# Expert weights loaded as one 16 KB run per partition in a two-layer mixture-of-experts kernel

## The reference

```
g = sel.reshape(sel.shape[:-1] + (N_GROUPS, EXPERTS_PER_GROUP))      # 16 experts in 4 groups
...
_, idx = lax.top_k(masked, TOP_K)                                    # 2 experts for each token
...
for e in range(N_EXPERTS):
    hid = jax.nn.silu(h @ w_gate[e]) * (h @ w_up[e])                 # (256,1024) @ (1024,512), twice
    out = out + gate[..., e:e + 1] * (hid @ w_down[e])               # (256,512) @ (512,1024)
```

## Time and profile before

| what | value |
|---|---|
| median of three runs | 2164.47 us |
| the profiled execution's own time | 2157.56 us |
| its span, first to last instruction | 2155.8 us |
| mean granted TensorE clock | 0.888 of full speed |
| TensorE matmuls busy | 1800.6 us |
| VectorE busy | 833.1 us |
| ScalarE busy | 460.8 us |
| DMA packets | 153206, 348.00 MB |
| DMA rate over the span | 161 GB/s |

### The profile page before, as it was taken

One profiled execution on the slowest core, in us unless ns is written; L12 is line 12 of the kernel. 1 busy time (PEld: TensorE's weight loads), 2 busy tenths in 40 slices (PEclk: granted clock), 3 DMA queues, 4 the chain that ended last, 5 costly groups with the idle time before them and its releaser, 6 DMA issues.

```text
span 2155.8 us, 23213 instructions
## 1 busy us (share of the span) xinstructions
PE 1800.6 (84%) x9255; PEld 1241.6 (58%) x9259; DVE 833.1 (39%) x1792; ACT 460.8 (21%) x812; POOL 0.4 (0%) x6
## 2 busy tenths in 40 slices
PE   6868899999695799999679876776789988687998
PEld 5545444434564454344265555775389984447998
DVE  7943211101404311001263465555255553505665
ACT  1031111111113111111011421110134430313443
POOL 0000000000000000000000000000000000000000
PEclk9858899999895889999879768887989998888999
DMA  8051379999304238999920000001525434101551
GB/s 278 0 215 52 107 269 393 396 395 356 128 30 185 90 131 311 396 392 395 342 101 27 1 1 0 1 1 37 198 73 196 160 120 153 40 0 40 182 208 59
DMA packets 153206, 348.00 MB, mean 161 GB/s; under 512 B 8096, under 2 KB 15136, under 8 KB 153136
## 3 DMA queue, kind: packets, MB, share of 16 engines
q1 hardware_dynamic: 145616, 338.28, 42.6%
q10 hardware_dynamic: 7520, 8.75, 1.3%
HBM read 345.97 MB, written 1.05 MB: 161 GB/s over the span
## 4 chain that ended last, share of the span: by engine, by line
PE 66%; DVE 13%; DMA 10%; issue 4%; ACT 4%; SPq 2%; another core or an unknown queue 1%; DVEq 1%; ACTq 0%
PE ps L690 62%; DMA ring<-in_w_up 9%; DVE ring L1634 2%; SPq L601 2%; DVE arena L1634 2%; DVE bias L1640 1%; DVE h L1640 1%; PE ps L964 1%; PE ps L697 1%; ACT arena L1444 1%; PE ps L1007 1%; DVE small L1640 1%; DMA arena<-in_rel_bias 1%; ACT hT L1277 1%
## 5 line engine op out<-in xcount | busy, mean ns | idle before, releaser
L690 PE MATMUL ps<-ring,arena 128*64 128x512 f32 (+3 forms) x1656 | 382.3, 595 | 25.3 <-DMA ring<-in_w_up 21.8
L690 PE MATMUL ps<-ring,hT 128*128 128x512 f32 (+5 forms) x864 | 355.0, 572 | 12.1 <-DMA ring<-in_mla_w_ukv 8.6
L690 PE MATMUL ps<-arena_r,ring_r 128*128 128x272 f32 (+1 forms) x1024 | 294.2, 287 | 0.0
L690 PEld LDWEIGHTS ps<-ring,arena 128*64 128x64 f32 (+1 forms) x1656 | 136.3, 145 | 255.4 <-issue 250.8
L690 PEld LDWEIGHTS ps<-ring,hT 128*128 128x128 f32 (+1 forms) x864 | 158.8, 186 | 201.3 <-issue 176.8
L1277 ACT ACTIVATE arena<-ps 128x256 f32<-128x256 f32 (+6 forms) x184 | 82.9, 478 | 634.5 <-PE ps L690 400.5
L690 PEld LDWEIGHTS ps<-arena_r,ring_r 128*128 128x128 f32 x1024 | 196.0, 191 | 0.0
L690 PE MATMUL ps<-arena_r,ff_hi_r 128*128 128x272 f32 (+1 forms) x992 | 186.2, 285 | 2.8 <-DVE arena L1634 2.8
L690 PE MATMUL ps<-arena_r,y_r 128*128 128x272 f32 (+1 forms) x544 | 152.6, 292 | 26.5 <-DVE ring_r L1634 23.4
L690 PE MATMUL ps<-arena 128*128 128x512 f32 (+9 forms) x460 | 134.4, 474 | 42.7 <-DVE small L1637 21.5
L690 PE MATMUL ps<-ring 128*128 128x128 f32 (+2 forms) x848 | 133.5, 325 | 40.2 <-DVE ring L1634 30.3
(11 more groups left out here) (262 smaller groups left out, 1701.8 us busy)
## 6 DMA issues: line engine op xcount, KB each, us to landing
ring<-in_w_down SPq DMA_DIRECT2D x32, 2048.0 KB, 14.5
ring<-in_w_gate SPq DMA_DIRECT2D x32, 2048.0 KB, 17.2
ring<-in_w_up SPq DMA_DIRECT2D x32, 2048.0 KB, 19.3
ring<-in_w_ff SPq DMA_DIRECT2D x32, 2048.0 KB, 8.2
ring<-in_w_in SPq DMA_DIRECT2D x8, 2048.0 KB, 19.7
ring<-in_w_in_ab SPq DMA_DIRECT2D x5, 2048.0 KB, 12.9
ring<-in_w_o SPq DMA_DIRECT2D x4, 2048.0 KB, 11.6
ring<-in_ple_gate SPq DMA_DIRECT2D x4, 2048.0 KB, 19.7
```

The costliest lines, as they stand in the source:

```text
L690: return pe.matmul(o, lhsT, rhs, start=a, stop=z)
```

## The change

The expert weights are dealt in runs of neighbouring rows: partition p receives rows 8p to 8p+7 of w_gate and w_up, and rows 4p to 4p+3 of w_down. For each partition these rows lie in one piece of 16 KB in HBM and go to 16 KB in one piece in SBUF. To match, piece k of the activations consists of every 8th column of h, beginning at k, and piece f of the hidden values of every 4th column, beginning at f. In bytes, neighbouring columns of a stationary operand are then 32 B apart in h and 16 B apart in hid, where they were 4 B apart. All of xT, hidT, the ring, the order of the instructions and every wait are as before.

```diff
+        h_rows = h_t[:, :].rearrange("p (t r k) -> p t r k", r=P, k=KC)
...
+        hid_rows = hid.rearrange("p (r k) -> p r k", k=FC)
...
-                    sp.dma_start(slot(n, k), A[name][l, d].rearrange("(k p) n -> p k n", p=P)).then_inc(slot_full[n], 16)
+                    sp.dma_start(slot(n, k), A[name][l, d].rearrange("(p k) n -> p k n", p=P)).then_inc(slot_full[n], 16)
...
-                                src = A[name][l].rearrange("e (k p) n -> e p k n", p=P)[bass.ds(i * 2 + d, 1)].rearrange("e p k n -> (e p) k n")
+                                src = A[name][l].rearrange("e (p k) n -> e p k n", p=P)[bass.ds(i * 2 + d, 1)].rearrange("e p k n -> (e p) k n")
...
-                            ins = mm(ps[:, 5 - c0 // 4, c * P:(c + 1) * P], h[:, t, (c0 + c) * P:(c0 + c + 1) * P], pick[:, t, :], t == 0, t == NT - 1)
+                            ins = mm(ps[:, 5 - c0 // 4, c * P:(c + 1) * P], h_rows[:, t, :, c0 + c], pick[:, t, :], t == 0, t == NT - 1)
...
-                            ins = pe.transpose(ps[:, 6, f * P:(f + 1) * P], hid[:, f * P:(f + 1) * P], ident)
+                            ins = pe.transpose(ps[:, 6, f * P:(f + 1) * P], hid_rows[:, :, f], ident)
```

## The result

The changed kernel takes 2205.72 us (median; 2203.12 to 2207.37) against 2164.06 us for the kernel before, run beside it. The ratio is 1.0184, with a 95% interval of 1.0169 to 1.0198. I had forecast 2133.5 us and a range up to 2190: wrong in sign, and outside the range. The rival "strided loads become the bound" is what happened, at a higher price than its upper end.

What follows compares the result with a forecast made beforehand. TensorE held 66% of the chain, but the loads' rate set the late expert turns, costing 31.0 us. Part 1's -31.0 plus part 2's 0 took the median 2164.47 to 2133.5 us; range 2127 to 2190 us.

Steps and rivals of the forecast that it cites:

- strided loads become the bound: Gathers and hid transposes: TensorE needs 32.3 us a turn, more than the loads' 31.9; +27.8 us, 2192 us; chance 0.26.
- upper end: Gather at half the clock, 6.72 us instead of 3.82 (+2.90); with hid's transposes (+0.4), +3.3 us a turn.
- What bounds the kernel: Expert stages: the loads' rate sets the late turns, about 31.9 us against TensorE's 29.02; slow loads cost 31.0 us.
- Part 1, packets and rate: Expert weight loads: 16 KB packets at 431 GB/s, turn at TensorE's 29.02 us, no w_up waits; -31.0 us.
- Part 2, the strided operands: Stationary loads of h and hid in gather and hid transposes: stride taken to cost 0.
- the point from which it decides: Stationary loads of h and hid: 31.0 us over 640 loads, 48 ns each, from which the change turns slower.
- hid's stride: Four transposes of hid, columns 16 B apart: taken as 0, at most +0.4 us a turn.

Runs made afterwards that it cites:

- small-packet kernel: Changed kernel's loads without each row's last 4 values, so rows don't join; gather and hid transposes read side by side: 2165.34 us, ratio 0.9988.
- stride experiment: Kernel before, with the gather's 8 pieces given stationary columns 1 to 8 values apart or moving columns 4 and 8 apart: 2176.88 us, single run.
- stride-only kernel: Strided reads of h and hid as in the change, with the DMA patterns of the kernel before: 2205.61 us, ratio 1.0194.
- kernel with pairs: Changed kernel, but w_gate and w_up dealt in runs of two rows (4 KB), h read 2 values apart, no copy: 2138.46 us, ratio 0.9859.

## Why the prediction was wrong

**What bounds the kernel** was right. 31.0 us were put on slow loads; the changed loads alone gave 33.3 us by their median, with an interval of about 27 to 39.

**Part 1, packets and rate** was right in each number: 83574 packets (about 83,600 forecast), 430 GB/s (431), and with the changed loads alone a turn of 29.01 us (29.02) and no wait on w_up. The small-packet kernel shows that the cause is the one that I gave.

**Part 2, the strided operands** is the step that failed: "I take 0, the value nearest to the rows at full clock, because the load's pace is half of what the moving side gets from the same memory." The price is 126 ns a load at full clock, for the 32 loads of each of 16 gathers; the two gathers ahead of the loops, which began at half the clock in both kernels, cost 1.20 and 2.62 us more. My reason compared two paces that were both measured side by side, with 4 values in each line. Neither of them says what a read pays that finds one value in a line. The stride experiment shows it: moving columns pay about the same as stationary ones when each is on its own line (225 and 230 ns). The comparison also set one load against two matmul records at a time. A single moving operand of 512 columns is no faster than a load, as the scatter of the kernel before shows: 3.60/8 = 0.45 us a record, 0.88 ns a column.

```profile
358.54 3.60 PE L690 MATMUL ps<-arena 128*128 128x512 f32 x8
```

**The upper end** failed too, and so the range. I bounded the price by the gather at half the clock, 6.72 us. The changed kernel's first gather ran at a mean granted clock of 0.59 and took 7.92 us, the later ones at 1.00 took 7.86. The strided load's time hardly moved with TensorE's clock, so a row at half the clock bounds nothing here. The row was misread as well. The earlier trace rows shows the clock only up to 281 us, and before that gather ended the clock had risen:

```profile
283.00:285.40 2.40, 2.40 (x17) 2.40 (x15) 0.21 (x1) 1.16 (x1) 0.00 (x0) 0.69 0.00 0
```

The 6.72 us are therefore a mixture. At half the clock throughout, my estimate from the earlier trace rows is 2 x 3.82 = 7.64 us, as the transposes of h in the earlier trace rows with their 215 against 109 ns also suggest. With +3.82 in place of +2.90 for each of the 18 gathers the rival would have come out at 2192 + 18 x 0.92 = 2209 us. That would have been near the measured time by luck, since the load's price has another cause than the clock. I had no row of a strided load, and should have set an end from a mechanism, one line for each column in place of a quarter, up to four times a side-by-side load. Instead I took the largest number that a row offered.

**The rival** "strided loads become the bound" had the right place, and the point from which it decides (48 ns) stands: 126 is far above it. It was priced 13.7 us too low: 4.07 us a turn instead of 3.3 is 0.77 x 16 = 12.3 us. For the two gathers ahead of the loops it had 5.8 us and 5.5 were measured, by luck, since 1.7 of them are the clock. Its chance of 0.26 was too small for a cost of which I said that no row tells it. It had seen that TensorE would need longer for a turn than the loads' 31.9 us. In that case the change's whole benefit is hidden, which the stride-only kernel shows (2206 us with either kind of loads).

**hid's stride** cost 0.4 us a turn in my upper end and 0.03 in the trace.

## What to carry to other kernels

A layout that makes transfers contiguous moves its stride to somebody else; price the reader of the stride before counting the gain. Count the 16-byte lines that a weight load touches: with two float32 columns in a line the stride was nearly free, with one the load took twice as long, and runs of two rows, or one copy a layer by an idle engine, kept the gain of the packets (0.986) where runs of four and eight lost (1.018). And where the trace has no row of an operation, an upper end from another clock level is no bound: ask what resource would set the price.

## What the runs showed of the hardware

- In the gather's float32 matmuls a stationary load of 128 columns took about 1.8 ns for each 16-byte line that it touches, and 112 ns at the least: 112, 117, 172, 230, 225, 237 ns for columns 1, 2, 3, 4, 6, 8 values apart. At a mean granted clock of 0.59 a gather 8 values apart took as long as at 1.00 (7.92 and 7.86 us). Side by side it took 6.72 us when it began at 0.50 and 3.82 at 1.00.
- Moving columns 4 and 8 values apart cost 225 and 233 ns a record of 128 columns instead of 119.
- With h read 8 values apart instead of side by side a transpose took 10 ns more (120 against 110).
- VectorE copied 1024 columns with a source 8 values apart in 1.08 us, less than the 1.84 us that 1.8 ns for each column would make.
- Loads from HBM ran at 384 to 387 GB/s in pieces of 2 KB, 408 to 412 in pieces of 4 KB and 425 to 430 in pieces of 16 KB (the last over 16 to 40 us). One sum fits all three: for each of the 16 DMA engines about 75 ns for each 2 KB and 10 ns for each piece. Shorter stretches scatter more, up to 446 GB/s in 6 us of the kernel with pairs.
